# A gated mixer on one core: gates and both up-projections by token-major chunks, gates and convolutions in turn, norm roots moved behind transposed pieces

## The reference, cut to what matters

```python
proj = hn @ w_in
q, k, v, g_out, g_low, z, xbc, dt_raw, gate_a, gate_b = split_cols(proj, IN_SPLITS)
...
y_a = o.reshape(Bsz, L, GLA_VW).astype(hn.dtype) @ w_up_gla      # gated linear attention, 1024 wide
xbc = jax.nn.silu(causal_dwconv(xbc, conv_w, conv_b))            # 3072 wide, 4 taps
...
y = y.reshape(Bsz, L, SSD_D_INNER) * jax.nn.silu(z)              # 2048 wide
y = rmsnorm(y.reshape(Bsz, L, SSD_GROUPS, SSD_D_INNER // SSD_GROUPS), ...)
y_b = y.astype(hn.dtype) @ w_up_ssd
mixed = jax.nn.sigmoid(gate_a) * y_a + jax.nn.sigmoid(gate_b) * y_b
return (mixed @ w_out).astype(hn.dtype)
```

## Time and the profile before

| | |
|---|---|
| median of 3 runs | 1484.07 us (1483.16 to 1484.78) |
| profiled execution | 1482.92 us, its span 1481.1 us |
| instructions | 18068 |
| PE busy | 1350.5 us, 91% of the span |
| DVE, ACT busy | 1062.8 us (72%), 678.5 us (46%) |

### The profile page before, as it was taken

How to read it: one execution, slowest core, us unless ns; L and a number is a source line. 1 busy time by engine, 2 the same in 40 slices (tenths; PEclk the granted TensorE clock), 3 DMA queues, 4 the chain that set the end, 5 groups by cost and what they waited for, 6 DMA issues and landing times.

```text
span 1481.1 us, 18068 instructions
## 1 busy us (share of the span) xinstructions
PE 1350.5 (91%) x6689; PEld 975.0 (66%) x6689; DVE 1062.8 (72%) x2111; ACT 678.5 (46%) x1246; POOL 309.0 (21%) x267
## 2 busy tenths in 40 slices
PE   9999999999999888788687777778999999999998
PEld 9999989779895333333233333333498888998876
DVE  6977688766698876777777677665787665766664
ACT  7765976674553322222122222222464575645663
POOL 0000000020045555344444444542200000000000
PEclk9999999999999999899989998999999999999999
DMA  8454555456979999999999999999765556554542
GB/s 304 151 178 145 183 180 166 149 161 188 351 309 404 421 422 421 422 421 421 421 423 420 422 421 422 421 420 422 309 220 178 161 182 187 167 173 142 168 144 87
DMA packets 78631, 418.78 MB, mean 283 GB/s; under 512 B 8832, under 2 KB 9024, under 8 KB 45648
## 3 DMA queue, kind: packets, MB, share of 16 engines
q0 software_dynamic: 37008, 268.45, 43.7%
q1 hardware_dynamic: 41536, 149.17, 31.6%
HBM read 416.51 MB, written 1.08 MB: 282 GB/s over the span
## 4 chain that ended last, share of the span: by engine, by line
PE 58%; DMA 28%; DVE 9%; ACT 3%; issue 1%; POOL 1%; DVEq 0%; SPq 0%; POOLq 0%; ACTq 0%
PE ps L1133 14%; PE ps L1135 14%; PE ps L1134 14%; DMA SLAB<-in_peer_uv,C 14%; DMA AR<-in_peer_uv,C 13%; PE ps L1454 9%; DVE wlo L2092 1%; DVE SLAB L2395 1%; DVE AR L2395 1%; ACT whi L1632 1%; PE ps L1382 1%; ACT AR L1851 0%; POOL AR L2666 0%; DVE AR L2233 0%; PE ps L1366 0%
## 5 line engine op out<-in xcount | busy, mean ns | idle before, releaser
L2092 DVE TENSOR_TENSOR wlo<-raw,whi 128x1024 fp32r<-128x1024 f32 x246 | 299.2, 1222 | 147.3 <-ACT whi L1632 146.9
L1454 PE MATMUL ps<-SLAB,AR 128*128 128x512 f32 x520 | 256.7, 645 | 64.9 <-ACT AR L1851 64.9
L1632 ACT ACTIVATE whi<-raw 128x1024 fp32r<-128x1024 f32 x246 | 259.1, 1057 | 120.4 <-PE ps L1135 102.2
L1454 PE MATMUL ps<-AR 128*128 128x512 f32 x504 | 245.3, 637 | 52.4 <-ACT AR L1851 52.3
L1133 PE MATMUL ps<-XH,whi 128*128 128x256 f32 (+1 forms) x896 | 261.6, 292 | 0.6 <-DVE XL L2330 0.6
L1135 PE MATMUL ps<-XH,wlo 128*128 128x256 f32 (+1 forms) x896 | 254.2, 284 | 0.0
L1134 PE MATMUL ps<-XL,whi 128*128 128x256 f32 (+1 forms) x896 | 254.1, 284 | 0.0
L1454 PEld LDWEIGHTS ps<-SLAB,AR 128*128 128x128 f32 x520 | 104.7, 206 | 211.9 <-issue 123.1
L1454 PEld LDWEIGHTS ps<-AR 128*128 128x128 f32 x504 | 100.5, 204 | 191.6 <-issue 115.0
L2395 DVE CUSTOM_DVE_ANT_0 SLAB<-SLAB,AR 128x1024 f32<-128x1024 f32 x130 | 158.1, 1223 | 72.6 <-DMA SLAB<-in_peer_uv,C 72.6
L2666 POOL DMA_INDIRECT AR<-in_peer_uv,C x125 | 146.8, 1174 | 253.2 <-PE ps L1454 144.5
(11 more groups left out here) (414 smaller groups left out, 1720.6 us busy)
## 6 DMA issues: line engine op xcount, KB each, us to landing
raw<-in_stream SPq DMA_DIRECT2D x246, 512.0 KB, 4.1
AR<-in_stream SPq DMA_DIRECT2D x9, 512.0 KB, 7.2
AR<-scr SPq DMA_DIRECT2D x8, 512.0 KB, 4.9
SLAB<-in_peer_uv,C POOLq DMA_INDIRECT x130, 28.0
AR<-in_rows SPq DMA_DIRECT2D x4, 512.0 KB, 5.1
AR<-in_peer_uv,C POOLq DMA_INDIRECT x125, 28.3
AR<-in_con SPq DMA_DIRECT2D x1, 1280.0 KB, 8.6
AR<-in_xin SPq DMA_DIRECT2D x2, 512.0 KB, 9.6
```

Of the source, the lines that this page charges most:

```text
L1454: t = pe.matmul(ps[2 * i + half][:, :], d, rows_in[:, 512 * half:512 * half + 512], start=c == 0, stop=c == 127)
L1632: a.activation(in_two(whi[i % NS][:, :]), src, ACT.Copy).then_inc(*hi.up(i))
L2092: v.tensor_tensor(in_two(wlo[i % NS][:, :]), src, in_two(whi[i % NS][:, :]).bitcast(F32), ALU.subtract).then_inc(*lo.up(i))
```

## The change

Gates, `ya` and `yb` become token-major. `GA` and `GB` hold 2 halves of tokens x 1024 features instead of 8 pieces of features x 256 tokens, and `gate`, `ya` and `yb_add` work on 512 columns (8, 4 and 4 times instead of 16, 8 and 8). The 16 gate chunks and the 24 convolutions come in turn, `CONV_GATES`: four convolutions, then 16 times one gate chunk and one convolution, then four convolutions. A block of gates holds one pair of banks for four chunks, and the convolutions between use the other pair, the fourth one `pair[0]`, just evicted. `mix` becomes a step of PE too: two transposes of 128 x 128 for each of 8 pieces into banks 4 to 7, read there by ACT and DVE; the last four come beside the first chunks of `out`, and `gain_in` (two loads on SP) behind them. In z, root 2 goes behind the first four `yT`, which start two turns later, and root 3 behind `yT` 8 and 9. The weights of the stream are laid out to match; bytes and flops of the weights stay the same.

```diff
@@ -45,16 +45,19 @@
 RESCALED_FROM = 5
-GATES_XS = [0] * 6 + [1, 0] * 10 + [1] * 6
-
-
-def gates_and_xs():
-
-    at = [8240, 5136]
-    out = []
-    for which in GATES_XS:
-        out.append(("T", "w_in", at[which], 1, 1024))
-        at[which] += 128
+CONV_GATES = "cccc" + 16 * "gc" + "cccc"
+
+
+def convs_and_gates():
+
+    out, convs, gates = [], 0, 0
+    for which in CONV_GATES:
+        if which == "c":
+            out.append(("T", "w_in", 7184 + 128 * convs if convs < 8 else 5136 + 128 * (convs - 8), 1, 1024))
+            convs += 1
+        else:
+            out.append(("N", "w_in", 8240 + 512 * (gates // 4), 1, 1024, gates % 4))
+            gates += 1
     return out
@@ -433,34 +436,65 @@
-    at["steps"] = 2
-    yield from stream_T("conv", [16, 17, 18, 19, 20, 21, 22, 23], conv)
-    yield from silu()
-    side(first_side())
-
-    def gate_or_x(c, i, b):
-        name, f = c
-        if name == "gate":
-            yield say("gate", f, i, b)
-            yield from silu()
-            return
-        if f >= 8:
+    def conv_evicted(f, i, b):
+        if 8 <= f < 16:
...
-        if f % 4 == 3:
+        if f == 23:
+            yield from silu()
+            side(first_side())
+        elif f < 16 and f % 4 == 3:
...
-    gates, xs = [("gate", f) for f in range(16)], [("x", f) for f in range(16)]
-    yield from stream_T("gx", [(xs if which else gates).pop(0) for which in GATES_XS], gate_or_x)
+    def conv_chunk(f, b):
+        yield from next_chunk("T")
+        i = at["next"] - 1
+        for k in range(8):
+            yield say("T", "conv", i, b, k, k == 7, k == 7)
+            if k == 3:
+                while mid:
+                    yield from mid.pop(0)
+                yield from side_step(2)
+            if k == 5:
+                yield from side_step(3)
+        done.add(("used", i))
+        yield from conv_evicted(f, i, b)
+        yield from side_step()
+
+    def gates_chunk(blk, kk, pair):
+        yield from next_chunk("N")
+        i = at["next"] - 1
+        for tt in range(2):
+            yield from one_tile("gates", i, pair[tt], tt, kk, 8)
+            if kk == 3:
+                yield say("gate", blk, tt, i, pair[tt])
+            if tt == 0:
+                yield from side_step(2)
+                yield from side_step(3)
+        done.add(("used", i))
+        yield from silu()
+        yield from side_step()
+
+    at["steps"] = 2
+    convs = [16, 17, 18, 19, 20, 21, 22, 23] + list(range(16))
+    for b in (2, 3, 0, 1):
+        yield from conv_chunk(convs.pop(0), b)
+    for blk in range(4):
+        pair, others = ((2, 3), (0, 1)) if blk % 2 == 0 else ((0, 1), (2, 3))
+        for kk, b in enumerate((others[0], others[1], others[0], pair[0])):
+            yield from gates_chunk(blk, kk, pair)
+            yield from conv_chunk(convs.pop(0), b)
+    for b in (3, 2, 1, 0):
+        yield from conv_chunk(convs.pop(0), b)
...
-    yield from stream_T("ya", range(8), plain("ya"))
+    yield from stream_N("ya", 2, 8, plain("ya"))
...
-        for _ in range(3 if g == 0 else 1):
+        for _ in range(5 if g == 0 else 1):
@@ -482,42 +516,49 @@
         if (blk, tt) == (2, 1):
-            sides.insert(0, Strand(y_roots(2)))
+            sides.insert(1, Strand(y_roots(2)))
 
...
     done.add("z")
-    yield from until(("yT", 7))
+    yield from until(("yT", 9))
     yield say("y_root", 3)
...
 
-    def mix_all():
-        while mixed:
-            yield say("mix", mixed.pop(0))
-
     def mix_side():
-        for f in range(4):
-            while ("yb", f) not in done:
-                yield PAUSE
-            yield from mix_all()
-            yield PAUSE
-
-    def yb(f, i, b):
-        yield say("yb_add", f, i, b)
-        done.add(("yb", f))
-        mixed.append(f)
+        while ("yb", 0, 1) not in done:
+            yield PAUSE
+        for _ in range(2):
+            yield PAUSE
+        for k in range(4):
+            yield say("mix", k)
+            yield PAUSE
+
+    def mix_last():
+        yield PAUSE
+        yield PAUSE
+        for k in range(4, 8):
+            yield say("mix", k)
+        at["steps"] = 1
+        yield PAUSE
+        yield say("gain_in")
+
+    def yb(blk, tt, i, b):
+        yield say("yb_add", blk, tt, i, b)
+        done.add(("yb", blk, tt))
 
     def y_ready(f):
-        yield from until(("yT", f if f < 8 else min(15, f + 4)))
+        yield from until(("yT", min(15, f + 2)))
+
+    def mix_ready(k):
+        yield from until(("mix", k))
 
...
     at["steps"] = 2
-    yield from stream_T("yb", range(8), yb, kt=16, ready=y_ready)
+    yield from stream_N("yb", 2, 16, yb, ready=y_ready)
     yield from side_all()
-    yield from mix_all()
     pending += EXTRA
-    at["steps"] = 1
-    yield say("gain_in")
+    side(mix_last())
 
@@ -535,7 +576,7 @@
     side(first_half())
-    yield from stream_N("out", 2, 8, out)
+    yield from stream_N("out", 2, 8, out, ready=mix_ready)
     yield from side_all()
@@ -1404,8 +1443,16 @@
                 elif step == "yb_add":
-                    f, i, b = at
-                    free[b] = dve.of(("yb_gate", f))
+                    blk, tt, i, b = at
+                    free[b] = dve.of(("yb_gate", blk, tt))
+                elif step == "mix":
+                    k, = at
+                    b, f = 4 + k % 4, slice(128 * k, 128 * k + 128)
+                    on.wait_ge(*dve.of(("yb", k // 4, 1)))
+                    bank(b)
+                    pe.transpose(ps[b][:, 0:128], GA[:, 0, f], ident)
+                    pe.transpose(ps[b][:, 128:256], GA[:, 1, f], ident).then_inc(*side.up(("mix", k)))
+                    free[b] = dve.of(("mix", k))
                 elif step == "out_add":
@@ -2280,10 +2329,11 @@
                 elif step == "ya":
-                    f, i, b = at
-                    on.wait_ge(*prod.of((i, 1)))
-                    on.wait_ge(*act.of(("gate", f)))
-                    v.scalar_tensor_tensor(GA[:, f, :], GA[:, f, :], 1.0, ps[b][:, 0:TX], ALU.add, ALU.mult).then_inc(*dve.up(("ya", f)))
+                    blk, tt, i, b = at
+                    ga = GA[:, tt, 512 * blk:512 * blk + 512]
+                    on.wait_ge(*prod.of((i, tt)))
+                    on.wait_ge(*act.of(("gate", blk, tt)))
+                    v.scalar_tensor_tensor(ga, ga, 1.0, ps[b][:, :], ALU.add, ALU.mult).then_inc(*dve.up(("ya", blk, tt)))
 
@@ -2724,7 +2775,7 @@
                 elif step == "gain_in":
-                    on.wait_ge(*dve.of(("yb", 7)))
+                    on.wait_ge(*dve.of(("yb", 1, 1)))
                     sp.dma_start(GW, rows[0:1, B_FFN:B_FFN + 1024].broadcast_to([128, 1024])).then_inc(s_rows, 16)
```

More of the change, by code:

```diff
@@ L66, in tile_order @@
         ("N", "w_in", 2048, 2, 1024),
[L67 to L68 removed]
+        *convs_and_gates(),
+        ("N", "w_up_gla", 0, 2, 1024),
         ("N", "w_in", 3088, 4, 1024),
[L70 removed]
+        ("N", "w_up_ssd", 0, 2, 2048),
         ("N", "w_out", 0, 2, 1024),
@@ L84, in chunk_plan @@
     chunks = []
-    for kind, name, c0, n, k in tile_order():
+    for kind, name, c0, n, k, *parts in tile_order():
         width, rows = (128, 1024) if kind == "T" else (512, 256)
         group = 4 if kind == "T" and k > 1024 else 1
-        chunks += [(kind, name, c0 + width * (g + i), kk, k) for g in range(0, n, group) for kk in range(k // rows)
+        chunks += [(kind, name, c0 + width * (g + i), kk, k) for g in range(0, n, group) for kk in (parts or range(k // rows))
                    for i in range(group)]
@@ L1004, in build @@
         XSG = place("XSG", 24952, 2176).rearrange("p (b f t) -> p b f t", b=2, f=4)
-        GA = place("GA", 7120, 2048).rearrange("p (f t) -> p f t", f=8)
-        GB = place("GB", 9168, 2048).rearrange("p (f t) -> p f t", f=8)
+        GA = place("GA", 7120, 2048).rearrange("p (i c) -> p i c", i=2)
+        GB = place("GB", 9168, 2048).rearrange("p (i c) -> p i c", i=2)
         Y = place("Y", 11216, 4096).rearrange("p (i c) -> p i c", i=2)
@@ L1149, in tensor_program @@
             x, raw_x = features("low_x", 0, T), features("raw_x", 0, T, XH0, XL0)
-            moving = {"qkv": raw_x, "g": raw_x, "conv": x, "gx": x, "z": x, "ya": features("o_x", 8 * T), "yb": features("yT", y_at),
+            moving = {"qkv": raw_x, "g": raw_x, "conv": x, "gates": x, "z": x, "ya": features("o_x", 8 * T), "yb": features("yT", y_at),
                       "out": features("mix", 0, TX, MXH, MXL), "pq": features("h_turn", 0), "rope": features("tile_turned1", 0),
@@ L1219, in tensor_program @@
                     what, i, b, tt, k, last, ends = at
-                    xh, xl, ready = moving[what](k, 128 * tt + (NM if what in ("g", "z") else 0), 128)
+                    xh, xl, ready = moving[what](k, 128 * tt + (NM if what in ("g", "gates", "z") else 0), 128)
                     ws = slice(k % 2 * 512, k % 2 * 512 + 512)
@@ L1324, in tensor_program @@
                 elif step == "gate":
-                    f, i, b = at
```

(32 more changed lines are left out.)

12 lines of the change are left out of this document (5 added, 7 removed).

## The result

The changed kernel takes 1489.7 us (median; 1487.68 to 1493.01 us), the kernel before 1484.42 us on the same chip: a ratio of 1.0043, 95% interval 1.0032 to 1.0054, so slower by 0.4%. Two executions are left out of this, one of the changed kernel at 1676.37 us (mean granted clock 0.75 where the others have 0.97) and one of the kernel before at 3398.91 us. The profiled execution took 1487.68 us with a span of 1485.9, 4.8 more than before. So the forecast of 1485.9 was 3.8 us too low, and the time lies just above the range.

A forecast was written before the change was run, and what follows sets the result against it. It took PE's own program to bound the changed stage, 80 to 400 us. Savings, transposes and two waits summed to +1.8 us: 1484.7 for the profiled execution, 1485.9 for the median with 1.15 added; range 1480.5 to 1489.5.

The forecast's parts named there:

- the pair of banks: Gate blocks: no wait for the gate in `pair[0]`, but +2.8 us where the next block's first convolution takes that bank.
- a gate in `pair[0]` is late at every block: Gate blocks: a listed sign that the prediction is wrong; it expected no wait on these evictions.
- The bank of convolution 23: First change of gate block: PE waits 2.8 us for this bank's late eviction, bounds 1.9 to 4.1.
- The roots: In z: moving the norm roots saves 2.0 us at `yT` 4 to 7, costs 2.4 at piece 12.
- the sum: Whole kernel: -3.0 - 2.0 - 0.2 + 1.8 + 2.8 + 2.4 = +1.8 us.
- the second rival: Third change of block: convolution 7 is evicted late, PE waits 2.3 us more; +4.1, 1488.2 us; chance 0.25.
- PE's own program: Mixer matmuls without waits: -3.0 us for token-major chunks, -0.2 for shared slow restarts, +1.8 for added transposes.
- The transposes of `mix`: Turning token-major `GA`: 16 added transposes at 0.11 us each, +1.8 us together (1.6 to 2.0), no wait.
- the token-major chunks: Gates, `ya`, `yb`: 40 chunks go from 24 matmuls of 256 columns to 12 of 512, saving 3.0 us.
- 227 ns: Token-major chunks: a matmul time listed as showing the prediction wrong; it expected 0.232 us start to start.
- 40 x 0.03: Token-major chunks: the saving by the skill page's matmul times, given as 1.3 us; measured gaps were used instead.
- the upper bounds: Likeliest case: the high ends of the terms' bounds, said to give +4.8 us, or 1488.9 us.

The follow-up runs named there:

- Six: The changed kernel with the banks of gates and convolutions in rotation, so none is asked for again too soon; 1483.43 us, ratio 1.0002.
- eleven: The changed kernel with decays of group 0 only for heads 0 and 4 (output not the network's), to shorten ACT's row; 1484.64 us, ratio 1.0009.
- One: The changed kernel with the convolutions' banks reordered from the second block of gates on, first convolution taking others[1]; 1486.78 us, ratio 1.0024.
- Three: The changed kernel with the norm roots where the kernel before has them; 1488.57 us, ratio 1.0036.
- four: The changed kernel with only root 3 put back ahead of pieces 8 and 9 of `yT`; 1486.78 us, ratio 1.0024.
- seven: The changed kernel with banks in rotation, and roots and first piece of `yT` where the kernel before has them; 1481.46 us, ratio 0.999.
- Eight: The kernel of seven with the attention's strand one turn later; 1482.05 us, ratio 0.9989.
- nine: The kernel of Eight with the first piece of `yT` one turn later; 1482.44 us, ratio interval 0.9984 to 1.0002.
- ten: The kernel of nine with `ssd_state` one turn later; 1481.91 us, ratio interval 0.9982 to 1.0.

## Why the prediction was wrong, point by point

**The step that failed** is the first sentence on the pair of banks: "the gate there is evicted while PE does its other half, 1.4 us against at most 0.7 on ACT, so no wait". The 0.7 is how long an eviction takes once ACT comes to it. What counts is how long after the product ACT comes to it, and that was in the kernel before too: there convolution 5 was evicted 4.6 us behind the end of its product, from the same row of decays. Its last matmul on PE, then its eviction on ACT, in the kernel before:

```profile
178.26 0.29 PE L1135 MATMUL ps<-XH,wlo 128*128 128x272 f32 x1
```

```profile
182.95 0.56 ACT L1732 ACTIVATE AR<-ps,PAR 128x272 f32<-128x272 f32 x1
```

It cost nothing, because a bank came round only after three chunks. The change cut that slack to PE's other half, 1.4 us (2.3 with the transposes that stand there), and PE waited 3.25 us. Six, which gives the slack back, and eleven, which shortens the row, both remove this wait. The list of what would make the prediction wrong had "a gate in `pair[0]` is late at every block"; one of four was enough.

**The bank of convolution 23**: 2.8 predicted, 2.75 measured, at the place and by the chain named (gate at 129.33 on ACT, silu, squares, table, the predicated copies to 137.6 on DVE). One shows that it counts in full. This one was priced from the product's end to the last instruction of the queue; the step that failed was not.

**The roots**: the wait of 1.5 us at `yT` went (-2.0 predicted), 0.7 came at piece 8 and 1.95 at piece 12 (2.4 predicted for both). Net +1.1 where the sum has +0.4. Three, four and seven put the cost of the move at about 2 us: with the roots at their old place and the rest changed, `yT` 4 to 7 wait only 0.3 us in three and seven, so the -2.0 was hardly due to the move. Eight, with the attention a turn later, has the 1.5 us again.

**Convolution 7 before 8**, the second rival, came with 0.6 us, not 2.3. The wait for `gla_state` (1.0 us) was in no case: L1317 waits for a state whose update on DVE stands behind a convolution (124.37 to 125.85) that the new order has put there. In return the wait of 1.0 us at 196 us in the kernel before went, which was not in the sum either.

**PE's own program** did better than the sum. From start to start the waits grew by 10.25 - 2.55 = 7.7 us and the mixer by 4.6, so the program became 3.1 us shorter; the sum has -3.0 - 0.2 + 1.8 = -1.4. The transposes of `mix` cost what they should (0.23 us a piece alone, 0.88 for the last four, 1.8 in all, no wait). The difference is in the token-major chunks. In `yb` 66 matmuls of 512 columns in a row, after:

```profile
363.33 0.48 PE L1174 MATMUL ps<-whi,XH 128*128 128x512 f32 x1
...
378.18 0.40 PE L1176 MATMUL ps<-whi,XL 128*128 128x512 f32 x1
```

are 65 gaps in 14.85 us, 228 ns each, where the sum took 232.4 from the earlier trace rows; in `ya` the median gap is 227. Over the 24 chunks of both that is 288 x 0.0045 = 1.3 us of the 1.7; the other 0.4 stays open. The prediction named 227 ns as what would make it wrong, and here it was, on the fast side.

Two slips in the recorded sums changed nothing: 40 x 0.03 is 1.2, not 1.3, and the upper bounds add up to +4.8 only without the -0.2.

**The sum afterwards**, in which the program is what is left beside the waits: -3.1 (program) + 2.75 + 3.25 + 0.6 (banks) + 1.0 (`gla_state`) - 1.0 (the wait at 196) + 1.1 (roots) = +4.6, as the milestone says. The forecast was +1.8; the gate's bank, put at nothing there, took 3.25. Without it the mixer would have come to +1.4, but partly by luck, since the program's extra 1.7 us and the 1.0 at 196 cancel the unforeseen 1.0 (`gla_state`), 0.6 (convolution 8) and 0.7 (roots). The rest of the distance between the medians, 5.3 us in one set and 7.7 in the other, is most likely the clock behind the long waits; that was seen in profiles, and not separated in the timed runs.

## What to carry to other kernels

Before a buffer is asked for sooner, measure how late its evictions are in the kernel as it is, from the end of the product and not from the start of the eviction: slack that shows no wait may be in use. Where two kinds of chunks share banks, rotate all of them, so that the shortest time between two uses is as long as it can be; here that was 7.5 us between the medians for a change of four lines. And price what a wait brings besides its length: here the clock of what followed was often lower.

## What the runs showed of the hardware

In these profiles the granted clock fell only within or right behind waits of 1.8 to 3.9 us between 120 and 388 us, and not each time: of eleven waits of PE of 2.5 us or more between 130 and 195 us, in seven profiled executions, seven were followed by a stretch of 4 us at 0.50 to 0.70. Of six waits of 1.8 us, those at 331 us in six and at 317 in nine did the same, and four in other kernels didn't. It cost about 1 to 2 us each time: the same 24 matmuls took 4.19 instead of 2.98 us. The kernels with no wait over 1.6 us, seven, eight, ten and the kernel before, show 1.00 in every stretch of 4 us from 120 to 388 us.

Three-pass products of 512 columns ran at 227 to 228 ns in `ya` and `yb`, and at 232 to 234 ns in the gates and in `out` (the earlier trace rows has 232.4). Why the two differ wasn't tried.
